# One block instead of two for a hybrid attention and expert step, with the key and value columns of W_in issued by the sync queue

## The reference, cut to what matters

```python
u = rms_norm(h, norm_attn_g)
q_sb, k_sb, v_sb, q_fx, k_fx, v_fx, f = split(u @ w_in)     # w_in: 2048 x (6 * 1024 + 8)
logf = log_sigmoid(f + b_forget)
o_sb = stick_breaking(q_sb, k_sb, v_sb)     # heads 0..7; samples: keys of 16 pages each
o_fx = forgetting(q_fx, k_fx, v_fx, cumsum(logf))            # heads 8..15, softmax
h = h + concat(rms_norm(o_sb, g_sb), rms_norm(o_fx, g_fx)) @ w_out
u = rms_norm(h, norm_ffn_g)
# top-1 of 4 groups, top-2 of its 8 experts, per token
y = sum(gate[e] * (silu(u @ w_gate[e]) * (u @ w_up[e])) @ w_down[e])
h = rms_norm(h + y, norm_final_g)
```

## Time and profile before

| | us |
|---|---|
| median of 3 runs | 1610.4 |
| lowest, highest | 1608.38, 1613.99 |
| the profiled execution | 1617.14 |
| its span | 1615.2 |
| PE busy | 1275.5 (79%) |
| DVE busy | 668.7 (41%) |
| ACT busy | 230.6 (14%) |

### The profile page before, as it was taken

One profiled execution on the slowest core, in us unless ns is written; L12 is line 12 of the kernel. 1 busy time (PEld: TensorE's weight loads), 2 busy tenths in 40 slices (PEclk: granted clock), 3 DMA queues, 4 the chain that ended last, 5 costly groups with the idle time before them and its releaser, 6 DMA issues. The chain is left out here.

```text
span 1615.2 us, 24640 instructions
## 1 busy us (share of the span) xinstructions
PE 1275.5 (79%) x7826; PEld 811.5 (50%) x7827; DVE 668.7 (41%) x4780; ACT 230.6 (14%) x454; POOL 62.4 (4%) x107
## 2 busy tenths in 40 slices
PE   5996679887969889847999776789867787767782
PEld 3775356655646656514777432355434444334451
DVE  3544655666557657659734654020100000000004
ACT  2100101212202213211010021010110001100011
POOL 1000000000000000001000000000010000000000
PEclk8998789899979989967999885799998889988997
DMA  9868599999989999999989899999999999999974
GB/s 329 235 221 325 176 397 394 397 396 394 357 334 379 395 366 395 389 388 371 360 335 361 316 364 353 411 377 411 422 399 381 381 388 388 372 375 382 369 332 167
DMA packets 188252, 576.64 MB, mean 357 GB/s; under 512 B 28697, under 2 KB 88906, under 8 KB 170218
## 3 DMA queue, kind: packets, MB, share of 16 engines
q1 hardware_dynamic: 116432, 507.82, 81.2%
q10 hardware_dynamic: 67282, 58.55, 11.0%
q0 software_dynamic: 4432, 9.05, 1.7%
HBM read 568.74 MB, written 17.77 MB: 363 GB/s over the span
## 5 line engine op out<-in xcount | busy, mean ns | idle before, releaser
L129 DVE CUSTOM_DVE_ANT_0 ws<-ws,xgT 128x128 f32<-128x128 f32 x1792 | 386.5, 281 | 90.2 <-issue 36.5
L1877 PE MATMUL bank<-ws,xgT 128*64 128x256 f32 x1024 | 260.4, 419 | 108.2 <-DMA ws<-in_w_expert_up 104.6
L932 PE MATMUL bank<-xn,ws 128*128 128x264 f32 x1152 | 297.0, 414 | 58.3 <-DMA ws<-in_w_in 58.3
L932 PEld LDWEIGHTS bank<-xn,ws 128*128 128x128 f32 x1152 | 228.0, 203 | 156.5 <-DMA ws<-in_w_in 66.9
L1879 PE MATMUL bank<-ws,xgT 128*64 128x256 f32 x1024 | 260.6, 419 | 0.0
L1877 PEld LDWEIGHTS bank<-ws,xgT 128*64 128x64 f32 x1024 | 152.9, 152 | 205.8 <-issue 120.5
L2076 DVE COPY gu<-bank 128x256 f32<-128x256 f32 x32 | 13.6, 424 | 391.0 <-PE bank L1879 391.0
L917 PE MATMUL bank<-ws,PR 128*32 128x512 f32 x1024 | 150.7, 668 | 21.2 <-DMA ws<-in_cache_fox_v 17.5
L1879 PEld LDWEIGHTS bank<-ws,xgT 128*64 128x64 f32 x1024 | 152.7, 152 | 0.0
L129 DVE DVE_READ_ACCUMULATOR2_ANT Z<- 128x1 f32 x1792 | 137.0, 76 | 0.0
L1898 PE MATMUL bank<-ws,hT 128*32 128x512 f32 x1024 | 115.7, 604 | 12.7 <-ACT xgT L1975 12.5
(11 more groups left out here) (409 smaller groups left out, 968.9 us busy)
## 6 DMA issues: line engine op xcount, KB each, us to landing
ws<-in_cache_sb_k SPq DMA_DIRECT2D x128, 512.0 KB, 8.1
ws<-in_cache_fox_k SPq DMA_DIRECT2D x128, 512.0 KB, 10.1
ws<-in_cache_sb_v SPq DMA_DIRECT2D x128, 512.0 KB, 7.6
ws<-in_cache_fox_v SPq DMA_DIRECT2D x128, 512.0 KB, 9.9
ws<-in_w_expert_gate SPq DMA_DIRECT2D x32, 2048.0 KB, 17.8
ws<-in_w_expert_up SPq DMA_DIRECT2D x32, 2048.0 KB, 24.9
ws<-in_w_expert_down SPq DMA_DIRECT2D x32, 2048.0 KB, 25.8
ws<-in_w_in ACTq DMA_DIRECT2D x16, 2048.0 KB, 30.2
```

Source lines behind the costliest of these rows:

```text
L129: ins = dve.tensor_tensor_reduce(k, k, qb[:, (g * H + h) * HD:(g * H + h + 1) * HD], 1.0, 0.0, ALU.mult, ALU.add, Z[:, n % 2, g, h, t:t + 1])
L932: mm = pe.matmul(out[:, 0:T], w[:, c, m * P:(m + 1) * P], xn[:, c, :], start=(c == 0), stop=(c == KC - 1))
L1877: pe.matmul(bank[2 * k][0:SLOTS, 0:256], lhs, ws[:, wg, c * 256:(c + 1) * 256], start=(c == 0), stop=(c == KC - 1))
```

## The change

1. Blocks A and B become one. The programs of block A are now methods of a class `start`, called at the head of each engine's program in block B; the barrier between them, and SP's wait for the stores of logf, go (the wait stands at step 8 now). Block A's buffers can no longer share memory with block B's, so they lie in tiles that are idle at that time (`blk`, `PR`, `osum`, `zs`, `ts`, ...). POOL clears `PR` after the last read of `wf`.
2. The sticks' weights of sample 0 are computed within the former block A: ACT's three softplus operations between head 4 and head 5, two more matmuls (L579, L580) on PE between head 6 and `partial(7)`, the exponential before head 7. What is left after the last head is the softmax half; the copies of sample 1's queries stand behind it on ACT.
3. SP issues the key and value columns of W_in, after value page s and key page s + 20 for s = 7, 11, ... 67, when the second head of the slot has been copied (`evac`).
4. The norm weights move from ACT's queue to SP's, behind x. The router weights, loaded by ACT in 10240 runs of 32 or 16 bytes, are now 5 loads by SP in rows of 4 or 2 KB ahead of the first W_in chunk, turned by 36 transposes on PE and two copies on DVE. ACT issues the forget columns and biases after its copies of x.
5. Semaphores are shared among several producers (`fg`, `fgc`, `small`, `act_in`, `W`).

```diff
 # SP, in the loop over the steps
             for s in range(STEPS):
+                if s == 8:
+                    sp.wait_ge(A["lst"], 32)
                 if s >= 4:
                     load_value_page(sp, S, vring, value_caches, ptr, s, n_phys)
                 if s + LEAD < STEPS:
                     load_key_page(sp, S, kring, key_caches, ptr, s + LEAD, n_phys)
+                if s % 4 == 3 and 7 <= s < 8 * TURNS - 1:
+                    i = (s - 7) // 4
+                    sp.wait_ge(S["evac"], 2 * i + 2)
+                    which, phi = i % 2, i // 2
+                    c0 = (1 + which + 3 * (phi % 2)) * H * HD + 256 * (phi // 2)
+                    sp.dma_start((wk, wv)[which], w_in[:, :, c0:c0 + 256]).then_inc(S[("wk", "wv")[which]], 16)
...
 # ACT, projected
-                if i % 2 and phi + 1 < PHASES:
-                    if i == 1:
-                        load_w(wk, 1, phi + 1, "wk")
-                    else:
-                        load_w(wv, 2, phi + 1, "wv")
...
 # SP, start
+                for g in range(NG):
+                    sp.dma_start(wrow[g], a["w_router_expert"][0, g].rearrange("(c p) e -> c (p e)", p=P)).then_inc(A["wr_in"], 16)
...
                 sp.wait_ge(A["q_done"], 4)
                 q_chunk(6)
+                sp.wait_ge(A["fgc"], FG["lf"])
+                sp.dma_start(logf_p[0, 0].rearrange("(t p) h -> p t h", p=P), lf[:, 0:2, :]).then_inc(A["lst"], 16)
...
-                sp.wait_ge(A["lst"], 32)
-        actx.close()
-        done_with(nc, A)
...
 # ACT, between the copies of head 4 and head 5
+                act.wait_ge(A["hused"], PAGES)
+                own.step(nc.scalar.activation(zs[:, :], Z[:, 0, 0, :, :].rearrange("p h j -> p (h j)"), ACT.Abs, scale=SCALE))
+                own.step(nc.scalar.activation(zs[:, :], zs[:, :], ACT.Exp, scale=-1.0))
+                nc.scalar.activation(zs[:, :], zs[:, :], ACT.Ln, bias=1.0).then_inc(S["ssl"], 1)
...
 # PE, ahead of the steps
-            pe.wait_ge(S["pad"], 1)
+            start.tensor(pe)
+            sample_max(0)
+            pe.wait_ge(A["q_evac"], 12)
             broadcast_queries(pe, S, bank[4:8], lastq, qpart, 1)
-            sample_max(0)
-            sample_sums(0)
+            pe.wait_ge(S["diag"], 1)
+            pe.matmul(bank[CH][:, 256:256 + H], ones[0:H, :], diag[:, :], start=True, stop=True).then_inc(S["C2"], 1)
...
 # ACT, ahead of the steps
+            start.scalar(act)
+            act.wait_ge(S["zx"], 1)
+            nc.scalar.activation(PR[:, 1, :, 0:H].rearrange("p j h -> p h j"),
+                                 zx[:, :].rearrange("p (h j) -> p h j", j=PAGES), ACT.Exp).then_inc(S["w"], 1)
             copy_queries(nc, act, S, bank[4:8], qb, 1)
-            sample_softplus(0)
-            act.wait_ge(S["pad"], 1)
-            sample_weights(0)
```

More of the change, by code:

```diff
@@ new lines, in hybrid_step @@
+        sp_h = sb("sp_h", [P, H, PAGES + 1], where=bctx)
+        run = sb("run", [P, H, PAGES + 1], where=bctx)
+        ts = sb("ts", [P, H * PAGES], where=bctx)
+        zx = sb("zx", [P, H * PAGES], where=bctx)
+        tri_gt, tri_le, later, grow = ts, zr, zx, zs[0:48, :]
+        lfr, LFT, totb = (blk[:, i * 1024:(i + 1) * 1024] for i in range(3))
+        totb = totb.rearrange("p (h n) -> p h n", h=H)
+        rstd = osum[:, 0:T]
+        prf = PR[:, :, :, :].rearrange("p g t r -> p (g t r)")
@@ L263, in hybrid_step @@
[L263 to L272, removed]
+        wrow = [qo[:, :, :].rearrange("p a f -> p (a f)")[0:KC, g * 1024:(g + 1) * 1024] for g in range(NG)] + [xg[0:KC, 0:512]]
@@ L282, in chunk, with sync @@
             return ws[:, Q_SLOT[n], :].rearrange("p (c n) -> p c n", n=256)
-        with nc.Block() as block:
-            @block.sync
-            def _(sp):
+        class start:
+            def sync(sp):
                 def q_chunk(n):
                     c0 = (n // 4) * 3 * H * HD + (n % 4) * 256
-                    sp.dma_start(chunk(n), w_in[:, :, c0:c0 + 256]).then_inc(A[f"w{n}"], 16)
+                    sp.dma_start(chunk(n), w_in[:, :, c0:c0 + 256]).then_inc(W[Q_SLOT[n]], 16)
                 def key_half(i):
@@ L470, in _ @@
                 pe.wait_ge(A["g_in"], 64)
-                pe.transpose(bank[0][:, 0:48], grow[:, :], ident[0:48, 0:48]).then_inc(A["gt"], 1)
+                pe.transpose(bank[0][:, 0:48], grow[:, :], ident[0:48, 0:48]).then_inc(A["small"], 1)
+                pe.wait_ge(A["tev"], 5)
+                pe.wait_ge(A["wr_in"], 16 * (NG + 1))
+                for e in range(NE):
+                    g, i = divmod(e, EPG)
+                    pe.transpose(bank[3][:, e * KC:(e + 1) * KC], wrow[g].rearrange("c (p e) -> c e p", e=EPG)[:, i, :], ident[0:KC, 0:KC])
+                for g in range(NG):
+                    mm = pe.transpose(bank[2][:, g * KC:(g + 1) * KC], wrow[4].rearrange("c (p e) -> c e p", e=NG)[:, g, :],
+                                      ident[0:KC, 0:KC])
+                mm.then_inc(A["small"], 1)
                 pe.wait_ge(A["rc"], 1)
@@ L554, in _ @@
                 head(6)
+                pe.wait_ge(A["fgc"], FG["ctc"])
+                pe.wait_ge(S["ssp"], 1)
+                pe.matmul(bank[1][:, P:2 * P], tri_ge[:, :], sp_h[:, :, 1:PAGES + 1], start=True, stop=False)
+                pe.matmul(bank[1][:, P:2 * P], ones[:, :], run[:, :, 0:PAGES], start=False, stop=True).then_inc(A["fg"], 1)
                 partial(7)
```

211 lines of the change are left out of this document (116 added, 95 removed).

## The result

| | before | after |
|---|---|---|
| median of the runs, us | 1612.2 (4 runs) | 1594.8 (4 runs) |
| lowest, highest | 1608.38, 1621.61 | 1587.93, 1597.38 |
| the profiled execution, its span | 1617.14, 1615.2 | 1596.19, 1594.4 |

The changed kernel takes 0.987 of the time (95% interval 0.9835 to 0.9905), about 21 us less; 34 had been forecast. It was run again in a later series: 0.9882 (0.985 to 0.9915). The mean of the three, 0.9875 or 20 us, is the reference for the experiments.

A forecast was written before the change was run, and what follows sets the result against it. The kernel was taken as bound by its DMAs wherever they are full, with gaps at the boundary and in the steps. 0.8 + 0.4 - 22.3 - 13 = -34.1, so 1610.4 - 34 = 1576.4 us, range 1564 to 1598.

The forecast's parts named there:

- The first rival, *only the barrier counts: Removing the barrier gives the gain, the order of SP's queue nothing: 1589.4 us; chance 0.16.
- The third, 1595: Boundary's wait only changes its name: ramp and chain at worst give 15 us, W_in nothing; chance 0.06.
- the main case: All terms hold, 1576.4 us, with its own range of 1570 to 1590; chance 0.58.
- The start: Up to PE's first partials: router rows ahead of W_in's chunks delay the fourth by 0.8 us, bounds 0 to 2.
- the softplus: Block A: softplus on ACT hidden, its sums on PE cost 0.4 us, bounds 0 to 0.8.
- The boundary: Between blocks, 146 to 200 us: without the barrier pages flow earlier, -22.3 us, bounds 16.5 to 24.5 won.
- W_in on SP: Steps, 200 to 660 us: one queue delivers in order of use at 398 GB/s, -13 us, bounds 0 to 17 won.
- The rule of the Trainium skill: All engines' DMAs share 16 DMA engines, so moving W_in saves nothing and the whole gain is 21.1 us.
- After step 72 all engines are simply earlier by what was won.: Behind the steps, W_out, router and experts are issued as before; step 72 about 34 us earlier, gain kept.
- SP held at `evac`: Rival in the steps: SP waits for a head's copy before issuing W_in, DMAs idle, 1656 us; chance 0.06.
- W_in was late: Rival in the steps: key page s + 20 delays W_in's loads, PE's 52 us wait stays, 1589 us; chance 0.04.
- won behind step 68: Rival, 660 to 980 us: PE no longer thrown back, 10 us more won, 1566 us; chance 0.10.

The follow-up runs named there:

- e2: The kernel before, with its two blocks and barrier, only W_in's key and value columns issued by SP's queue: 0.9984 of the kernel before, 2.6 us less.
- e6: The changed kernel with nine small loads (gains and router rows) moved from SP's queue to ScalarE's: 0.9869 of the kernel before.
- e7: The changed kernel with DVE's sum of weights done behind page 16, value pages 4 and 5 issued behind key pages 20 and 21: 0.9861 of the kernel before.
- e5: The changed kernel with SP waiting for page 19's scores before issuing key page 20, at 172.09 us: 0.9904 of the kernel before.
- e1: The changed kernel with W_in's key and value columns issued by ScalarE again: 0.9904 of the kernel before, median 1600.6 us.
- e8: The changed kernel with W_in's loads cut as 4 rows of 1024 columns (4096 B), outputs not the reference's: 0.9775 of the kernel before.
- e11: The changed kernel with W_in in rows of 128 columns (512 B), two loads per slot, outputs not the reference's: 0.9981 of the kernel before.
- e9: The changed kernel with the edits of e6 and e7 together: 0.9892 of the kernel before.
- e4: The changed kernel with W_in's loads cut as 8 rows of 512 columns (2048 B), outputs not the reference's: 0.9856 of the kernel before.
- e10: The changed kernel with W_in issued by ScalarE in 4 rows of 1024 columns, outputs not the reference's: 0.9819 of the kernel before.

## Why the prediction was right or wrong, point by point

The sign was right, the time (1576.4) 18 us too low, inside the range (1564 to 1598) near its upper end. The first rival, *only the barrier counts* (1589.4), is nearest in its mechanism. The third, 1595, is nearest in its number, and that is luck: it has the boundary's chain at its worst, which came as forecast. That the time fell inside the range is owed to the width that the rivals gave it; the main case's own range, 1570 to 1590, missed.

- **The start (+0.8, with +0.4 for the softplus).** Not measurable as a whole. PE's last heads end at 113.05 + 35.76 = 148.8 against 146.1, 2.7 us later, and the table has 2.0 at 40 MB. But e2, whose first block is the one before, ends them at 112.63 + 35.76 = 148.4:

```profile
112.63 35.76 PE L499 MATMUL bank<-xn,ws 128*128 128x264 f32 x160
```

  Against e2 the changed kernel loses 0.4 us here, so the profiled execution before was an early one, and 0.4 to 2.7 us is all that can be said of a forecast of 1.2. The softplus cost nothing visible: ScalarE's copy of head 5 waits 0.23 us. One size was wrong: the fourth chunk, 2.9 us later than in the earlier trace rows and 2.6 later than in e2 (37.30), against a bound of 2:

```profile
39.88 2.36 PE L511 MATMUL bank<-ws,xn 128*32 128x256 f32 x20 [2.38 <-DMA ws<-in_w_in]
```

  My reason for it, rows on few partitions ahead of the chunks, is not what costs: e6 took them out of the queue and the chunk was no earlier. What may be left are the forget-gate columns, now issued beside the chunks (a DMA share of 1.16 at 325 GB/s from 20 to 28 us, 1.09 at 348 before); that was not tried.
- **The boundary (-22.3).** Right, step by step: key page 20 at 161.6 us (160.7 forecast), value page 4 at 173.4 (171.2), 21.6 us won between 40 and 60 MB. The window from 163 to 180 us moved 371 GB/s, so the DVE-paced pages cost the little that I had put in. PE's wait of 11.13 us for DVE's sum was not foreseen; by e7 it cost nothing. By itself, with the start's loss, the boundary is worth 15 to 18 us of time where the two terms give 21.1; in e5's trace such a difference shrinks in the steps, from 8.1 us to 6.4.
- **W_in on SP (-13).** This is the step that failed, the term that was put at 13 and measured 3 to 5, in "398 GB/s, no worse than the 401 of the two queues together". The signs beside it came as named: landing 21.5 us (under 25 forecast), PE's wait for W_in 6.7 (under 10). But the rate was 386 (393 or more forecast), and the time came out at 3 to 5 us by e1 and e2. I had read the PE wait as time to be won. It was the wait of a kernel whose DMA engines were full at a share of 1.02 on average, for all the short gaps around 478 us, and it went over to the value pages. The price of the pages was nearly right: 409 GB/s (205 to 220 us) where I took 413, so 8.39 MB are 20.5 us. 10.49 MB at the measured 386 are 27.2, which leaves 6.7 us for W_in's 2.10 MB, 313 GB/s and not 348; a part of that is the idle time behind a full queue. A base of 383 leaves no room for such an error: 15 GB/s were the term. The rows of 1024 B are what holds the rate down, as e8 and e11 show.
- **The rule of the Trainium skill** ("DMA: Bandwidth & Descriptors", "Issuing engines are not separate DMA queues"), by which the move saves nothing, was much nearer to the runs, 2.6 and 4.7 us, than my term. The other rule of the Trainium skill (the same page, "Queues, rings and completion order"), of turns between the queues, fits the landing (30.9 us in e1, 21.5 in the changed kernel) and not the time.
- **"After step 72 all engines are simply earlier by what was won."** Wrong as well. ACT's last copy of a projected head, at step 71, starts at 652.55 us against 683.80, 31 us earlier (34 forecast for step 72), and the span is 21 us shorter. So at step 72 the forecast looks nearly right, and a third of the lead is gone at the end, which I had named as a sign of being wrong. By bytes the lead was 25.9 us at 240 MB, 30.2 at 260 and 21.6 at 340. Between them PE is the bound, and an early start leaves the DMAs idle sooner:

```profile
740.00:880.00 140.00, 137.85 (x679) 104.16 (x677) 67.85 (x584) 14.14 (x30) 1.81 (x1) 1.00 0.87 326
```

  and before, in the same window:

```profile
740.00:880.00 140.00, 132.59 (x636) 99.34 (x633) 83.42 (x656) 15.91 (x29) 8.33 (x23) 0.95 0.95 362
```

  The three profiles of this kernel lose 8.6, 10.9 and 10.2 us from 260 to 340 MB, e11 loses 9.7, but e8 3.4 and e1 0.9, and e9, the same in time as this kernel, 2.9. That the loss lies in this stretch is seen; why it differs so, and what would keep the lead, was not tried.
- **The other rivals.** No sign of SP held at `evac`: its waits from 200 to 700 us are the two above, 9.3 us in sum for ring places, and none is for ACT. W_in was late by 6.7 us in sum and not by 52, and nothing was won behind step 68.

## What to carry to other kernels

Before a wait for one load is booked as gain, look at the DMA share of the stretch: here, at 1.02, the wait passed to the next load in line, and what was won was the change of rate. So compute that from rates that are measured over long windows of the same mix. Compare two profiles by when the same bytes have been moved, at several marks; a lead seen in one engine's steps may not be worth its size at the end. If the queue is full, cut the loads so that each run of bytes is longer before moving them between queues: here a cut to rows of 4096 B was worth 16 us and the move 3 to 5. (The kernel with that cut leaves out loading the right columns. A correct kernel would have to project four heads at a time from such rows, with buffers that this one doesn't have; it was not tried.)

## What the runs showed of the hardware

- A packet costs time beside its bytes: on each engine of SP's queue, over the range from 512 B to 4096 B, 9 to 11 ns by when the same bytes were moved (e4, e8, e11) and 8 to 12 by the packets' summed times. 369, 386, 394 and 402 GB/s were moved in 200 to 640 us with the same 33.6 MB, a fifth of that stretch's bytes, in rows of 512, 1024, 2048 and 4096 B.
- An engine can be held in the issue itself: 11.25 us for one value page of 512 KB behind a 2 MB load. I call the cause a full queue. With the same bytes in a quarter of the packets (e8) it is 3.7 us, so the room seems to be counted in packets. It shows as a long issue, not as a wait, so SP's waits from 200 to 700 us fell to 9.3 us, from 215 in the kernel before:

```profile
SPq L115 <- PE bank L917: 123.4, 34, 14.3
SPq L105 <- DVE Z L129: 91.9, 50, 7.0
```

- The landing of a 2 MB load changed with its queue and its rows: medians of 30.9 us on ScalarE's queue with rows of 1024 B (e1), 15.1 with 4096 B (e10), and 21.5 on SP's with 1024 B.
- The kernel before had 10240 packets under 512 B more, the router's (28697 against 18457). They cost share: from 50 to 60 us its DMA engines have a share of 0.64 for 72 GB/s, the changed kernel's 0.38 for 118. That this end of the small runs won any time doesn't show: at 40 MB the changed kernel is 2.0 us behind the one before and 0.3 behind e2.
